# HGRN outputs of a head, token tile by token tile, between the dense matmuls of a projection unit

## The reference, cut to what matters

```
def step(s, inp):                      # one chunk of 32 tokens, all heads
    qc, kc, vc, lf = inp
    lc = cumsum(lf); qt = qc * exp(lc); kt = kc * exp(-lc)
    a = where(tril, qt @ kt.T, 0)
    o = a @ vc + qt @ s                # the outputs
    s = exp(lc[-1]) * s + (kc * exp(lc[-1] - lc)).T @ vc
...
o = o * rsqrt(mean(o * o) + eps) * norm_g      # per token and head, 64 values
o = o * silu(gb)
```

## Time and profile before

| | us |
|---|---|
| median of 3 runs | 2359.87 (2358.88 to 2367.54) |
| profiled execution | 2370.57 |
| its span | 2368.8 |
| mean granted clock of TensorE | 0.952 |

### The profile page before, as it was taken

One profiled execution on the slowest core, in us unless ns is written; L12 is line 12 of the kernel. 1 busy time (PEld: TensorE's weight loads), 2 busy tenths in 40 slices (PEclk: granted clock), 3 DMA queues, 4 the chain that ended last, 5 costly groups with the idle time before them and its releaser, 6 DMA issues.

```text
span 2368.8 us, 33284 instructions
## 1 busy us (share of the span) xinstructions
PE 2184.4 (92%) x13978; PEld 1839.8 (78%) x13978; DVE 1095.9 (46%) x2104; ACT 742.6 (31%) x1374; POOL 76.1 (3%) x84
## 2 busy tenths in 40 slices
PE   7999989989779999996799999969999999999994
PEld 6986767769459999994788885448898898889883
DVE  2037787746422555575221112554444444444446
ACT  3226666635312545441111011222121122112117
POOL 0021000001100000000000000000000000000003
PEclk9998999989989998996899999979999999999997
DMA  9231000066641111102411113111111111111001
GB/s 251 58 133 28 10 11 1 10 224 198 213 135 45 37 29 38 30 10 72 124 37 54 27 45 124 36 36 54 54 45 45 37 62 45 36 54 45 27 18 72
DMA packets 148384, 154.65 MB, mean 65 GB/s; under 512 B 33482, under 2 KB 131875, under 8 KB 143500
## 3 DMA queue, kind: packets, MB, share of 16 engines
q1 hardware_dynamic: 142284, 116.06, 16.4%
q0 software_dynamic: 5952, 36.47, 4.5%
HBM read 136.95 MB, written 19.74 MB: 66 GB/s over the span
## 4 chain that ended last, share of the span: by engine, by line
PE 82%; DVE 7%; DMA 4%; ACT 4%; issue 2%; SPq 0%; POOL 0%; POOLq 0%; DVEq 0%; ACTq 0%
PE PS L716 53%; PE PS L1231 5%; PE PS L1205 4%; PE PS L916 3%; PE PS L983 2%; PE PS L897 2%; DMA arena<-in_cache_sel_kv,arena 2%; PE PS L869 1%; DVE arena L1691 1%; PE PS L968 1%; PE PS L1153 1%; DVE arena L1707 1%; PE PS L871 1%; DMA arena<-in_x_prompt 1%; PE PS L1141 1%
## 5 line engine op out<-in xcount | busy, mean ns | idle before, releaser
L716 PE MATMUL PS<-x_low,w_high_mlp 128*128 128x344 f32 x1152 | 370.8, 322 | 0.0
L716 PE MATMUL PS<-w_down_high,hidden 128*128 128x512 f32 x1024 | 328.6, 396 | 10.2 <-DVE arena L2178 5.8
L716 PE MATMUL PS<-x_high,w_high_mlp 128*128 128x344 f32 x768 | 246.8, 321 | 5.7 <-DVE w_low L737 5.7
L716 PE MATMUL PS<-x_high,w_low 128*128 128x344 f32 x768 | 247.1, 322 | 0.0
L716 PEld LDWEIGHTS PS<-w_down_high,hidden 128*128 128x128 f32 x1024 | 192.8, 188 | 68.0 <-DVE arena L2178 20.4
L2178 DVE TENSOR_TENSOR arena<-arena,PS 128x512 f32<-128x512 f32 x256 | 175.1, 686 | 142.3 <-PE PS L716 142.3
L716 PEld LDWEIGHTS PS<-x_low,w_high_mlp 128*128 128x128 f32 x1152 | 218.4, 190 | 2.6
L716 PE MATMUL PS<-w_down_low,hidden 128*128 128x512 f32 x512 | 201.5, 394 | 0.0
L716 PE MATMUL PS<-x_low,w_high_hgrn 128*128 128x344 f32 x576 | 189.5, 329 | 0.0
L716 PE MATMUL PS<-x_high_a,w_low 128*128 128x344 f32 x480 | 158.8, 331 | 0.0
L716 PE MATMUL PS<-x_high_b,w_low 128*128 128x344 f32 x480 | 154.0, 321 | 0.0
(11 more groups left out here) (343 smaller groups left out, 4041.7 us busy)
## 6 DMA issues: line engine op xcount, KB each, us to landing
wring<-in_w_in SPq DMA_DIRECT2D x100, 256.0 KB, 3.4
wring<-in_w_up SPq DMA_DIRECT2D x64, 256.0 KB, 3.3
arena<-in_w_down SPq DMA_DIRECT2D x16, 1024.0 KB, 5.0
arena<-in_x_prompt SPq DMA_DIRECT2D x16, 512.0 KB, 5.4
x_high_kept<-x_high_att SPq DMA_DIRECT2D x1, 4128.0 KB, 14.5
arena<-in_cache_win_kv SPq DMA_DIRECT2D x8, 512.0 KB, 4.9
arena<-in_w_out SPq DMA_DIRECT2D x2, 2048.0 KB, 8.8
out<-arena SPq DMA_DIRECT2D x8, 512.0 KB
```

The source lines that it names most:

```text
L716: mm = pe.matmul(out, w, x, start=(start and k == 0 and i == 0), stop=(stop and k == tiles - 1 and i == 2))
```

## The change

The outputs of an even head are issued inside its out-gate unit, those of an odd head (1, 3, 5) inside the forget-gate unit of the next head: `unit_and_outputs` issues one token tile (`out_tile`) after every second k tile of the second and third chunk, that is after every six dense matmuls. The wait for the recurrence goes with the first tile. Head 7's outputs stay in one piece. `turn_out` of the odd heads moves behind the next head's q unit. On VectorE the copy, squares and sum of an odd head (`out_squares`) go ahead of the next head's masked copies and the scaling (`out_normed`) ahead of its recurrence; `turned_out` goes behind the recurrence; the split of the next weights goes ahead of the recurrence. On ScalarE the factors of an odd head go between the next head's key copies and state copies, those of an even head behind the copy of the out-gate unit. The order of the steps, `wsteps`, follows. The diff, cut:

```diff
+        wsteps = []
+        for h in range(HG):
+            wsteps += [(h, s) for s in range(8)]
+            if h and h % 2 == 0:
+                wsteps += [(h - 1, 9), (h - 1, 10)]
+            wsteps += [(h, 8)]
+        wsteps += [(HG - 1, 9), (HG - 1, 10)]
...
+            def out_tile(h, t):
+                if t == 0:
+                    pe.wait_ge(*copied(wstep(h, 3)))
+                    pe.wait_ge(s_s, NCH * (h + 1) - 1)
+                    wbank(h, 8)
+                out = PS[:, 3 + wstep(h, 8) % 5, DV * t:DV * (t + 1)]
+                mm = pe.matmul(out, atm[:, t, :], vt[:, t, DV * h:DV * (h + 1)], start=True, stop=False, skip_group_check=True)
+                for j in range(4):
+                    c = 4 * t + j
+                    if c:
+                        mm = pe.matmul(out[CH * j:CH * (j + 1), :], qT[:, h % 2, CH * c:CH * (c + 1)], Sb[:, c - 1, :],
+                                       start=False, stop=True, skip_group_check=True)
+                if t == NQ - 1:
+                    mm.then_inc(w_ps, 1)
+
+            def unit_and_outputs(n, h):
+                pe.wait_ge(w_in_s[n % WR], 32 * (n // WR + 1))
+                pe.wait_ge(wl_dve, n + 1)
+                for ci, (c0, cn) in enumerate(CHUNKS):
+                    x = 3 * n + ci
+                    pe.wait_ge(u_act, x - 2)
+                    for k in range(KD):
+                        mm = split_product(pe, unit_out(x, P, cn), [whH[:, n % 2, k, :]], [wl[:, n % WR, k, :]],
+                                           [x_high(k)[:, c0:c0 + cn]], [xl[:, k, c0:c0 + cn]], start=(k == 0),
+                                           stop=(k == KD - 1))
+                        if k == KD - 1:
+                            mm.then_inc(u_ps, 1)
+                        if ci and k % 2:
+                            out_tile(h, 4 * (ci - 1) + k // 2)
+
             for h in range(HG):
-                if h + 1 < HG:
+                if h and h % 2 == 0:
+                    unit_and_outputs(unit_f(h + 1), h - 1)
+                elif h + 1 < HG:
                     unit_matmuls(pe, unit_f(h + 1))
-                if h >= 1 and h % 2 == 0:
-                    turn_out(h - 1)
...
+                if h and h % 2 == 0:
+                    turn_out(h - 1)
                 if h % 2 == 0:
-                    unit_matmuls(pe, unit_g(h // 2))
+                    unit_and_outputs(unit_g(h // 2), h)
+                elif h == HG - 1:
+                    for t in range(NQ):
+                        out_tile(h, t)
             turn_out(HG - 1)
...
-                for s in (0, 1, 4, 5, 6, 7):
+                for s in (0, 1):
+                    step_copy(h, s)
+                if h and h % 2 == 0:
+                    rms_factors(h - 1)
+                for s in (4, 5, 6, 7):
                     step_copy(h, s)
...
                         split_high(act, unit_g(h // 2) + 2, whH[:, unit_g(h // 2) % 2])
+                    rms_factors(h)
+            rms_factors(HG - 1)
...
-                if h >= 1 and h % 2 == 0:
-                    turned_out(h - 1)
+                if h and h % 2 == 0:
+                    out_squares(h - 1)
                 for s in (2, 3):
...
                     ins.then_inc(w_dve, 1)
+                n = unit_q(h + 1) + 1 if h + 1 < HG else U_M
+                if n < U_M:
+                    split_low(dve, n, n, whH[:, n % 2])
+                if h and h % 2 == 0:
+                    out_normed(h - 1)
 
                 for c in range(NCH):
...
+                if h and h % 2 == 0:
+                    turned_out(h - 1)
                 if h + 1 < HG:
-                    n = unit_q(h + 1) + 1
-                    if n < U_M:
-                        split_low(dve, n, n, whH[:, n % 2])
                     prepare(h + 1)
...
+                if h % 2 == 0 or h == HG - 1:
+                    out_squares(h)
+                    out_normed(h)
             turned_out(HG - 1)
```

More of the change, by code:

```diff
@@ L492, in hybrid_step @@
         BY_ACT = (0, 1, 4, 5, 6, 7)
+        wsteps = []
[5 more added lines that the diff above has]
+        wsteps += [(HG - 1, 9), (HG - 1, 10)]
+        step_at = {hs: i for i, hs in enumerate(wsteps)}
         def wstep(h, s):
[L496 to L500, removed]
+            return step_at[h, s]
         def copied(i):
@@ L1482, in decay, with rms_factors @@
                 act.activation(lcb, lcb, ACT.Exp).then_inc(he, 1)
+            def rms_factors(h):
+                act.wait_ge(lb_s, h + 1)
+                ra(act.activation(hsm[:, 8:16], hsm[:, 0:8], ACT.Ln, scale=1.0 / DV, bias=hsm[:, 95:96]))
+                ra(act.activation(hsm[:, 16:24], hsm[:, 8:16], ACT.Exp, scale=-0.5))
             decay(0)
@@ L1975, in prepare, with out_squares, out_normed @@
                 dve.wait_ge(hk, h + 1)
+            def out_squares(h):
+                i = wstep(h, 8)
+                dve.wait_ge(w_ps, i + 1)
+                dve.tensor_copy(osb, PS[:, 3 + i % 5, :].rearrange("p (t v) -> p t v", t=NQ)).then_inc(w_dve, 1)
+                dve.wait_ge(*copied(i))
+                hv(dve.tensor_tensor(sqb, osb, osb, ALU.mult))
+                dve.tensor_reduce(hsm[:, 0:8], sqb, AX.X, ALU.add).then_inc(lb_s, 1)
+            def out_normed(h):
+                dve.wait_ge(r_act, 2 * (h + 1))
+                if h % 2 == 0 and h >= 2:
+                    dve.wait_ge(w_ps, wstep(h - 1, 10) + 1)
+                dve.tensor_tensor(onb[:, :, DV * (h % 2):DV * (h % 2 + 1)], osb,
+                                  hsm[:, 16:24].unsqueeze(2).to_broadcast([P, NQ, DV]), ALU.mult).then_inc(on_s, 1)
+                dve.wait_ge(on_s, h + 1)
             prepare(0)
```

3 lines of the change are left out of this document (removed).

## The result

The changed kernel takes 2350.73 us (median of 6 runs, 2344.00 to 2353.25) against 2361.98 us of the kernel before on the same chip (6 runs, 2358.88 to 2367.54): a ratio of 0.9944, 95% interval 0.9927 to 0.9962. That is 11 us less, and the interval does not reach 1. Timed once more beside the kernel before it took 2349.73 against 2365.12 us, 0.9938 (0.9923 to 0.9953). In the experiments one execution of the kernel with the norms moved alone took 8437 us against 2350 to 2355 of the five others; its ratio leaves that one out, its median counts it, and nothing recorded says why it was slow.

The account below looks back on a forecast made before the run. PE, busy 92% of the span, was taken as the bound. Seven stretches gain 22.6 us, less 1.0 and 3.1 for new waits, less 2.9 for one fall fewer: 15.6 off 2359.87 gives 2344.3 us, range 2338 to 2355.

Parts of the forecast that it names:

- The sum: Whole kernel: 22.6 us gained in seven stretches, less 1.0 and 3.1, makes 18.5; one fall less leaves 15.6 us.
- The stretches: First seven heads, from the unit before the outputs to the next short block: 170.85 us becomes 148.2.
- Waits of 0.59 us: PE time lost ahead of the outputs in each of seven heads, 4.1 us together, expected to go.
- A tile at 0.61 us, not 0.72: Each output token tile among dense matmuls, its first weight load taken as hidden; 56 tiles make 34.4 us, otherwise 40.3.
- the rival of the dear tiles: First weight load of each tile not hidden, 0.72 us a tile; 5.9 us less gain, 2350.2 us; chance 0.18.
- Heads 2, 4, 6: Short blocks where moved VectorE sums delay the masked copies: PE waits 0.3 us more, three times, 1.0 us.
- Head 7: Head 6's norm delays state products from 3.08 to 5.95 us: 2.9 us lost, plus 0.2 for a clock fall.
- The clock: Seven mixed units hold full clock because dense matmuls stand between tiles; all 17.9 us of falls and stalls go.
- 14.6 us of falls gone: Half-clock stretches during the outputs of five of seven heads, about 2.9 us each, expected to vanish.
- Norms: Moved sums, factors and scaling, nothing added; at full clock they keep ScalarE from holding the unit copies, a 2.71 us stall.
- One fall less for the median run: Correction from profiled execution to median run: 2.9 us taken off the 18.5 us gain, leaving 15.6.
- the rival of the few falls: Ordinary runs of the kernel before have no falls but pay stalls; gain 10.1 us, 2349.8 us; chance 0.16.

Follow-up runs that it names:

- one-piece runs: Changed kernel with all eight token tiles undivided in the unit: after the second chunk's sixth dense matmul 2349.29 us, after the unit's first six 2346.95 us.

## Why the prediction was right or wrong

The range (2338 to 2355) holds the 2350.73 us, the direction and the main sums held; the reason given for one term did not.

- *The sum.* The stretches were to take 148.2 us and took 147.9. Waits of 0.59 us gone in seven heads: right. A tile at 0.61 us, not 0.72: right, with the first weight load hidden as behind the turns. So the rival of the dear tiles is out. By the rule of the Trainium skill ("TensorEngine Tiling (Array Packing)", Key Properties) that a changed tiling mode drains TensorE, divided and undivided outputs make equally many changes; their stages took 265.9 us both.
- *Heads 2, 4, 6.* State products were to start 3.3 us behind the block's start; they start at 3.2 (PE idle 0.34 us instead of 0.18). The price was 0.5 us in all, not 1.0.
- *Head 7.* State products at 5.95 us: they start at 6.00. For a fall of the clock in the new idle time 0.2 us were taken; it cost 1.3 in one profile and nothing in the other, inside the bounds 0 and 2.
- *The clock, the step that failed.* "Between tiles there are now six dense matmuls" was given as the reason why nothing falls. The one-piece runs show that the outputs hold full clock undivided as well, once nothing idle stands ahead of them; the two heads among them that had a moment at the place of falls are the evidence. The two heads that had held it in the profile before were no sign of that: they had the same idle time, and their moments lay at 0.36 and 0.42 us. The remark in the sum that falls depend on where the outputs lie against the clock's decisions was right. The term (14.6 us of falls gone) was right in size all the same, since each of the seven waits went with the move.
- *Norms.* They were costed as a way to avoid stalls of 3 us. With them alone the stage is already at 270.3 to 273.2 us, 15 to 18 of the 22.7 us gained in the first profiles; part of that is luck, since falls stayed possible and only one came. Against the profile without a fall the place of the outputs brings another 4.4 us, most of it the waits, and takes away what makes falls possible; dividing them brings nothing.
- *From the profile to the median.* The profile's stage up to the merge gained 17.9 us (359.92 to 342.07) against 18.5 in the sum. "One fall less for the median run" was the wrong correction: a fall that is missing in an even head is a stall instead, and three profiles of before, with five, three and two falls, agree within 2 us. That also answers the rival of the few falls. The medians gained 11.3 and 15.4 us, with intervals that reach from 9 to 18. The rest of the distance lies in what varies outside the stage; the profiles of one kernel differ by up to 9 us before it starts.
- *The slower rival*, clock lost in mixed units, found no support: 1.00 in each of them, and no idle time at the changes between PSUM banks, so that the rule of the Trainium skill ("TensorE: Matmul & The Clock Gate", A second HAM failure mode), by which such idle time makes the clock swing, finds nothing here to act on.

## What to carry to other kernels

Before dividing a run of small matmuls among dense ones to hold the clock, try the run undivided with its wait covered: put it a few dense matmuls later, so that no idle time precedes it. When an engine is held in its queue by a wait for a result that nobody needs yet, move that wait behind the work that others need, and look at who stands last when the loop ends: the last turn has no unit behind it to hide what was moved. Where a fall of the clock and a stall stand in for each other, price them together. And before calling a kernel free of falls from one profile, see whether any of its stretches met the clock at the place where others fell.

## What the runs showed of the hardware

A run of 4.8 us of matmuls with 64 columns, most of them on 32 columns of weights, holds the full 2.4 GHz when dense work runs into it without a gap (14 of 14 heads, two of them with a moment of the clock at the place of falls), and loses it in 13 of 40 when 0.43 us of idle time precedes: in all 13 with such a moment 2.77 to 3.36 us behind the start, and in none of the 27 with it at 0.29 to 2.27. A fall costs near 2.9 us here: 6.8 us at 1.2 GHz. Idle time of 2.71 us ahead of dense matmuls was followed by a fall in three stalls of five in the kernel before, for 3.4 us each. Behind 3.1 us of idle time on PE the state products ran at 1.2 GHz in one profile (3.33 us) and at 2.4 GHz in another (2.01). An fp32 matmul starts 0.16 us behind a dense one as if it were one of them, while the first dense matmul behind fp32 ones costs 0.105 us more, wherever it stands.
